# The first gather of a mixture-of-experts layer reads unscaled rows, and a ninth weight unit is loaded into the room of the scaled copy

## What is computed

```python
h = x + merge_heads(...)                       # 288 tokens x 2048
xn = h * rsqrt(mean(h*h) + EPS) * g_ffn_norm   # rms_norm
g_sel = argmax(xn @ w_rg + b_rg)               # one of 4 groups
top_v, top_i = top_k(expert logits of that group, 2)
gate = g_prob * softmax(top_v)
for each expert e (32 of them), rows xb = xn[its tokens]:
    y[its tokens] += gate * ((silu(xb @ w_gate[e]) * (xb @ w_up[e])) @ w_down[e])
h = h + y
```

## Time and profile before

| | us |
|---|---|
| median of three runs | 1785.23 |
| the three runs | 1783.72, 1785.23, 1787.71 |
| the profiled execution, its own time | 1790.77 |
| its span, first to last instruction | 1789.1 |
| PE busy | 1434.1 (80%) |
| DVE busy | 473.3 (26%) |
| ACT busy | 206.5 (12%) |
| POOL busy | 83.3 (5%) |
| DMA moved | 555.31 MB, mean 310 GB/s |

### The profile page before, as it was taken

The page is one execution under the profiler, slowest core; times in us unless marked ns, Lnnn a source line. Parts: engine busy times, 40 slices in busy tenths (PEclk is TensorE's granted clock), DMA queues, the critical chain, the costliest instruction groups (busy, mean ns, idle before and its releaser), DMA issues.

```text
span 1789.1 us, 22896 instructions
## 1 busy us (share of the span) xinstructions
PE 1434.1 (80%) x9330; PEld 798.3 (45%) x9330; DVE 473.3 (26%) x1217; ACT 206.5 (12%) x478; POOL 83.3 (5%) x147
## 2 busy tenths in 40 slices
PE   7999999999999999998767665866576567666646
PEld 6877777776777454455332231412223113122111
DVE  3106674552135666203002011011020110200201
ACT  3010101002332222113000000000000000000000
POOL 2000000220001322000000000000000000000000
PEclk9999999999999999998888888888888878878868
DMA  7643244342258999853899999999999999999996
GB/s 258 193 122 98 72 139 141 123 138 80 71 174 304 379 399 378 303 214 141 334 425 420 428 425 427 429 429 429 430 429 429 429 429 429 429 428 429 428 427 224
DMA packets 120617, 555.31 MB, mean 310 GB/s; under 512 B 11839, under 2 KB 65184, under 8 KB 94752
## 3 DMA queue, kind: packets, MB, share of 16 engines
q1 hardware_dynamic: 112080, 517.75, 72.4%
q0 software_dynamic: 8464, 36.54, 5.7%
HBM read 545.32 MB, written 8.72 MB: 310 GB/s over the span
## 4 chain that ended last, share of the span: by engine, by line
PE 64%; DMA 29%; DVE 3%; issue 1%; ACT 1%; SPq 1%; POOL 1%; DVEq 0%; POOLq 0%; ACTq 0%
PE PS L1859 22%; PE PS L2439 16%; DMA arena<-in_w_up_e_dram 9%; DMA arena<-in_w_down_e_dram 9%; DMA arena<-in_w_gate_e_dram 8%; PE PS L2480 7%; PE PS L2297 4%; DMA arena<-in_cache_fox_k_dram 2%; PE PS L2279 1%; PE PS L1913 1%; PE PS L2211 1%; PE PS L2398 1%; PE PS L2414 1%; PE PS L1847 1%; DVE arena L1537 1%
## 5 line engine op out<-in xcount | busy, mean ns | idle before, releaser
L2439 PE MATMUL PS<-arena 128*32 128x512 f32 x1792 | 291.5, 733 | 194.5 <-DMA arena<-in_w_up_e_dram 125.6
L1859 PE MATMUL PS<-arena 128*128 128x288 f32 (+1 forms) x1728 | 445.2, 406 | 1.0 <-ACT arena L996 0.5
L1859 PEld LDWEIGHTS PS<-arena 128*128 128x128 f32 x1728 | 320.8, 191 | 93.6 <-issue 20.9
L2439 PEld LDWEIGHTS PS<-arena 128*32 128x32 f32 x1792 | 70.4, 131 | 406.5 <-issue 195.1
L2480 PE MATMUL PS<-arena 128*32 128x512 f32 x872 | 136.8, 708 | 117.1 <-DMA arena<-in_w_down_e_dram 117.1
L2439 PE MATMUL PS<-front,arena 128*32 128x512 f32 x256 | 145.8, 735 | 0.0
L2480 PEld LDWEIGHTS PS<-arena 128*32 128x32 f32 x872 | 36.9, 127 | 210.8 <-issue 119.8
L1773 DVE TENSOR_TENSOR arena<-arena,PS 128x512 f32<-128x512 f32 x8 | 5.5, 687 | 401.8 <-PE PS L2439 401.8
L1783 DVE TENSOR_TENSOR arena<-arena,PS 128x512 f32<-128x512 f32 (+1 forms) x96 | 65.6, 683 | 157.9 <-PE PS L2414 157.9
L2398 PE MATMUL PS<-arena 128*128 128x128 f32 x768 | 94.3, 283 | 1.7 <-DVE arena L1747 1.7
L2398 PEld LDWEIGHTS PS<-arena 128*128 128x128 f32 x768 | 90.5, 197 | 9.7 <-issue 7.5
(11 more groups left out here) (365 smaller groups left out, 1291.6 us busy)
## 6 DMA issues: line engine op xcount, KB each, us to landing
arena<-in_w_gate_e_dram SPq DMA_DIRECT2D x56, 2048.0 KB, 15.0
arena<-in_w_up_e_dram SPq DMA_DIRECT2D x53, 2048.0 KB, 15.2
arena<-in_w_down_e_dram SPq DMA_DIRECT2D x53, 2048.0 KB, 15.3
arena<-in_cache_fox_v_dram POOLq DMA_DIRECT2D x64, 384.0 KB, 9.0
arena<-in_w_in_dram SPq DMA_DIRECT2D x6, 3072.0 KB, 10.8
front<-in_w_gate_e_dram SPq DMA_DIRECT2D x8, 2048.0 KB, 23.0
front<-in_w_up_e_dram SPq DMA_DIRECT2D x8, 2048.0 KB, 23.5
arena<-in_cache_fox_k_dram SPq DMA_DIRECT2D x40, 384.0 KB, 11.1
```

The lines of the kernel that those rows point to most:

```text
L1859: last = pe.matmul(PS[0:m, bank, 0:w], wt[:, k, c:c + m], rhs[:, k, :], start=(k == 0), stop=(k == KC - 1))
L2439: last = pe.matmul(PS[x * SLOTS:(x + 1) * SLOTS, which, :], xgT[:, kk, x * SLOTS:(x + 1) * SLOTS], wt[:, k, :], start=(kk == 0), stop=(kk ...
```

## The change

Five things are edited together.

1. The first gather (round 0) reads `h_tok` itself, in the strided order of `in_halves`, and multiplies it with `pick_first`, which is `pick_tok` times `rstd`. DVE makes it with three instructions right behind `pick_pair(0)`.
2. The scaled copy is made later, behind `units_used` 2: two instructions of ACT ahead of its first `pair_act`, one of DVE within `pair_dve(0)`. TensorE waits for them (`h_scl` 4) before it gathers for round 1.
3. The room of the copy, `HSC`, holds `ahead2` first, a ninth place for a unit, in which (1, 0) is loaded behind `wo_filled` 9. `pick_first` stands behind it.
4. The place that (1, 0) had is free, so (2, 1) is loaded into it at once, ahead of the wait on `half_used`, and no longer behind `units_used` 2.
5. POOL's clearing of tile 2 is gone, and every gather uses 32 rows of the third tile instead of 128.

```diff
+        ahead2 = view(HSC, UNIT)
+        pick_first = view(HSC + UNIT, 3, XQ, SLOTS)
...
             load_wo_rest(3, wo_in[2])
+            sp.wait_ge(wo_filled, 9)
+            sp.dma_start(ahead2.rearrange("p (k n) -> p k n", n=FFW), w_gate_r[0, 1]).then_inc(group_in[1], 16)
             sp.wait_ge(wo_filled, NWO)
-            for x in (0, 2):
-                load_first(1, x)
+            load_first(1, 2)
 
             sp.wait_ge(lg_filled, NWO)
             sp.dma_start(ahead.rearrange("p (k n) -> p k n", n=FFW), w_gate_r[1, 1]).then_inc(group_in[1], 16)
+            load_unit(0, 2, 1)
...
             for g in range(2, GROUPS):
-                for x in ((1,), (2, 3, 1), (0, 2, 3, 1), (0, 2, 3, 1))[g - 2]:
+                if g == 2:
+                    sp.wait_ge(units_used, g)
+                for x in ((), (2, 3, 1), (0, 2, 3, 1), (0, 2, 3, 1))[g - 2]:
...
-            pool.wait_ge(wo_filled, 9)
-            pool.memset(h_scaled[:, 2, :], 0.0).then_inc(consts_set, 1)
...
-            scale_rows(0, P)
-            scale_rows(1, P)
             for n, (o, i) in enumerate(((rw[:, :, 0:NG], rw[:, :, 0:NG]), (rw[:, :, 60:61], rw[:, :, 60:61]))):
...
+            act.wait_ge(units_used, 2)
+            scale_rows(0, P)
+            scale_rows(1, P)
             with act.Fori(0, QUADS - 1) as p:
                 pair_act(p)
...
-            dve.wait_ge(consts_set, N_CONSTS + 1)
-            dve.tensor_scalar(by_half(h_scaled[0:NS, 2, :]), in_halves(h_tok[0:NS, 2, :]), rstd[0:NS, 7:8], None, ALU.mult).then_inc(h_scl, 1)
...
+            def first_picks_scaled():
+                dve.wait_ge(picked_set, 1)
+                for t in range(3):
+                    ins = dve.tensor_scalar(pick_first[:, t, :, :], pick_tok[:, t, :, :], rstd[:, 5 + t:6 + t], None, ALU.mult)
+                ins.then_inc(h_scl, 1)
...
                 if not last:
                     dve.wait_ge(pg_set, p + 1)
                     pick_pair(p + 1)
+                if first:
+                    dve.wait_ge(units_used, 2)
+                    dve.tensor_scalar(by_half(h_scaled[0:NS, 2, :]), in_halves(h_tok[0:NS, 2, :]), rstd[0:NS, 7:8], None, ALU.mult).then_inc(h_scl, 1)
...
             pick_pair(0)
+            first_picks_scaled()
             gate_values()
...
-            def gather(p, chunks):
+            def gather(p, chunks, now=False):
 
                 for c in chunks:
                     o = PS[:, 2 + c // 4, (c % 4) * P:(c % 4 + 1) * P]
-                    for t in range(3):
-                        last = pe.matmul(o, h_scaled[:, t, c * P:(c + 1) * P], pick_tok[:, t, :, :].rearrange("p x s -> p (x s)"),
-                                         start=(t == 0), stop=(t == 2))
+                    for t, (t0, w) in enumerate(TILES):
+                        if now:
+                            h, picks = in_halves(h_tok[0:w, t, :])[:, c // 8, c % 8, :], pick_first
+                        else:
+                            h, picks = h_scaled[0:w, t, c * P:(c + 1) * P], pick_tok
+                        last = pe.matmul(o, h, picks[0:w, t, :, :].rearrange("p x s -> p (x s)"), start=(t == 0), stop=(t == 2))
...
-                                wt = ahead if first and (g, x) == (1, 1) else group_unit(g, x)
+                                wt = {(1, 1): ahead, (1, 0): ahead2}.get((g, x), group_unit(g, x)) if first else group_unit(g, x)
...
                         if g == 2 and not last_pair:
                             pe.wait_ge(picked_set, p + 2)
-                            if not first:
+                            if first:
+                                pe.wait_ge(h_scl, 4)
+                            else:
                                 pe.wait_ge(part_added, p * NPART)
                             gather(p + 1, range(8))
...
-            pe.wait_ge(picked_set, 1)
-            pe.wait_ge(h_scl, 3)
-            gather(0, range(5))
+            pe.wait_ge(h_scl, 1)
+            gather(0, range(5), True)
```

More of the change, by code:

```diff
@@ L2424, in pair_pe @@
                         if first and g == 1:
-                            gather(0, range(9, KC))
+                            gather(0, range(9, KC), True)
                         pe.wait_ge(group_in[g % 3], p * 128 + (64 * (g // 3) + 64))
@@ L2432, in pair_pe @@
                                 last.then_inc(half_used, 1)
-                                gather(0, range(5, 9))
+                                gather(0, range(5, 9), True)
                             if first and which == 0 and k % 4 == 0:
```

## The result

The changed kernel takes 1801.26 us in the median of six runs (1800.18 to 1804.35), the kernel before 1786.29 (six runs, the three from before the change among them): ratio 1.0086, 95% interval 1.0073 to 1.0099. It is slower by some 15 us where 7.4 us less were forecast, and outside the range. The profiled execution has a span of 1802.7 us against 1789.1.

The account below looks back on a forecast made before the run. Experts' weights stream at memory speed, 428 to 430 GB/s, while TensorE waits. One unit less (4.9 us) and a closed gap (3.1) make 8.0; with later events 7.4 remain, so 1785.23 - 7.4 = 1777.8 us, range 1776 to 1786.

Parts of the forecast that it names:

- 9.9 - c: Gain in us once C holds the stream of weight loads; the forecast c of 2.5 gave 7.4.
- c: Delay of event C caused by the change, forecast as 2.5 us.
- C: Event on TensorE when group 1 is done, 872.99 us in the kernel before, on which loads hang; forecast at 875.5.
- The gap closes: Before group 3's loads: (3, 1) is issued while earlier loads still come, so 3.1 us of idle stream go.
- the copy is covered: Before round 1's gather: ACT's late scalings, 7.97 us, delay nothing, as group 3's unit comes 5 us after that gather.
- TensorE need not stop after C: Between groups 1 and 2: with (2, 1) already loaded, group 2 follows directly and ends near 882 instead of 892.68.
- rival 3: At group 3's end: the gap opens one group later, up to 3 us lost again, 1781 us; chance 0.08.
- I take the pace as 0.147: First gather's strided load and matmul pairs: 0.147 us each, adding 0, 0.8 and 1.4 us in the three sets.
- sign of being wrong: Third set of first gathers, 42 strided loads: taking 10 us or more, where about 6.2 was forecast.
- rival 2: First gather's strided loads: 0.25 us each loses 0.6 us (1785.8), 0.294 a pair loses 4.9 (1790.1); chance 0.16.
- 1 (a load that does not hide): All 96 strided loads of the first gather: 0.093 us more per pair, c = 9.2, time 1784.5; chance 0.22.
- A: Event on TensorE when half of group 0 is done, 854.48 us in the kernel before, on which loads hang; forecast 0.3 later.

Follow-up runs that it names:

- E1: Changed kernel, but the first gather reads 128 neighbouring columns of h_tok (round 0 multiplies permuted rows): 1788.12 us, ratio 1.0005 to the kernel before.
- F2: Changed kernel, columns still 32 bytes apart, but with 128 rows of the third tile: 1786.75 us, ratio 0.9993 to the kernel before.
- F1: E1 with all 128 rows of the third tile in every gather: 1779.17 us, ratio 0.9945 to the kernel before.
- F3: Kernel before with 32 rows instead of 128 for the third tile in every gather, nothing else: 1794.9 us, ratio 1.0032.
- F4: F1 with round 0's weight rows placed to match contiguous columns of h_tok, gain applied in that order: 1782.74 us, ratio 0.9965 to the kernel before.
- E3: Changed kernel with the first gather's columns 8 bytes apart (round 0 multiplies permuted rows): 1790.27 us, one run.
- E4: Changed kernel with the first gather's columns 16 bytes apart (round 0 multiplies permuted rows): 1798.32 us, one run.
- G2: F4 with two neighbouring weight rows in a partition (4 KB pieces) and columns 8 bytes apart: 1782.81 us, ratio 0.9970 to the kernel before.

## Why the prediction was wrong

**The stream, the ninth unit and the formula were right.** Gain = 9.9 - c gives -14.2 for the c of 24.05, and the time rose by 15.0. For E1 the profile's C is 8.8 us later, counted from the first gather; with the 0.6 us of later start the formula gives a gain of 0.5, measured a loss of 0.9 with an interval that reaches to a gain of 0.7. For F2 it gives 0.1, measured about 1.2. With gathers as quick as before the sum of the prediction is 4.9 + 3.1 = 8.0, and F1 gained 8.5. "The gap closes" and "the copy is covered" hold in F1, and "TensorE need not stop after C" within 0.6 us (C at 872.16, group 2 at 872.78); the cover is gone in E1, whose gather for round 1 is slow.

One margin in the prediction mixes two counts: the "4.2 us" that the group before had in rival 3 leave out the 1.66 us from event to flow, which the two microseconds beside it include; with them it is 2.6. The time does not hang on it.

**Three steps failed, and all are terms of c.**

1. *"The third tile's 32 rows instead of 128 change no column count, so nothing."* This is the step that no rival covered. By itself it takes 8.9 us of C (E1 against F1) and 5.7 to 7.2 us of the time in the kernel before (F3). Of the 8.9 the half group behind the first set and the small matmul are 2.1, at the low clock of point 3. I priced the instruction and not the sequence: the gathers alternate between two forms, and before each change of form the loads stand still (0.22 us at half clock, F3).

2. *"I take the pace as 0.147."* Measured 0.24 at 128 rows (F2): 9.3 us of C where 2.2 were forecast. The third set in the changed kernel took 13.50 us, beyond the 10 that the prediction named as its sign of being wrong. Rows 6 were the wrong neighbour. They are a transpose, whose load is shorter to begin with (140 ns against 192), at 24 bytes. Near the mark was ScalarE's 0.25, the first price of rival 2, at the same 32 bytes and from the same tensor. I had that row, called it a bound and gave it 0.16 together with a worse one. Overlap of loads with matmuls, on which I leaned, is real at 113 ns; a strided load of 335 ns still comes every 243 ns (F2), so part of it is hidden and more than the forecast is not.

3. *The clock was no term at all.* The prediction took the half groups between the sets as fixed. After the change they took 6.05 and 6.12 us for the 3.6 of before, at a granted clock of 0.59 and 0.58 on average, 0.50 for the most part, with PE fully "busy". Summed: the sets give (10.19 - 6.46) + (7.47 - 2.99) + (13.50 - 4.89) = 16.8 us of c, the two half groups (6.05 - 3.57) + (6.12 - 3.64) = 5.0, group 1 1.3, the small matmul between (L2523) 0.4, and the later start 0.6: 24.1 in all. Taken one at a time stride and rows give 9.3 and 8.9, 18.2 together, but both at once 23.6 (52.2 - 28.6). Of the 5.4 us over their sum 4.6 lie in the half groups and group 1, which take (6.05 - 5.28) + (6.12 - 3.57) + (8.36 - 7.07) more than in E1, at the low clock. So either edit alone, contiguous columns (E1) or 128 rows (F2), gives back 14 to 15 us of c. In F2 the clock was 1.00 from 848 on, with pairs of 0.24 us; with pairs of 0.31 it fell again during the second and third sets.

In E1 and F3, with no stride, the clock stayed at 0.50 through the first set, at 0.31 us a pair, and once it was at 1.00 the second and third sets kept it at 0.176. In every profile whose clock stayed down through the first set, or fell in the second or third, the gathers have the 32-row form; no run has pairs of 0.31 us with 128 rows. So slow pairs and the form itself are not told apart, and the cause in the chip stays open. What it cost is measured.

Of the rivals, 1 (a load that does not hide) had a price of 0.093 more per pair and 1784.5; the stride costs 0.13. Rival 2 had the right place, the 66 loads between A and C, and nearly the right first price, but gave 1785.8, a loss of 0.6 us, because it lacked terms 1 and 3; F2, with these two out, measures level with the kernel before (0.9993). Its second price, 0.294 a pair, gave 1790.1, nearer to 1801.26, but by a double reading of the operand that F2's 0.24 does not bear out. The point it named, c = 9.9, is where F2 and E1 stand, and both measure as no change.

## What to carry to other kernels

Price what a change does to the sequence of forms on TensorE, not only each instruction: cutting the third tile's operand from 128 rows to 32 made every chunk of six pairs 0.35 us longer at full clock, and padding with zeros was faster. Where a stationary operand would be read more than 8 bytes apart in float32, give the slowest strided read of the same tensor on any engine a good chance as its price (one match here: ScalarE's 0.25 us, TensorE's 0.24), or change the row order of the other operand (F4) so that the read is contiguous. And where a stream of loads hangs on three events of one engine, the gain is bounded while the loss is not: here 8 us could be won and each further microsecond on that engine was paid nearly in full (c 24.05, time 15.0 up, against 9.9 - c).

## What the runs showed of the hardware that was not expected

- Changing between loads of 128 and of 32 rows leaves 0.22 to 0.23 us idle at each change at 1.2 GHz (F3). At 2.4 GHz an estimate is 0.18, half of the 0.35 that a chunk with two changes is longer.
- A stationary float32 operand with columns 8 bytes apart costs 0.007 us per 128 columns (E3), at 32 bytes it costs 0.13 (F2), and at 16 bytes the third set is as long as at 32 (13.54 and 13.50 us, E4 and the changed kernel).
- The granted clock was 0.50 over 12 us in which PE counts as busy all the time and no engine was waited for: "busy" in a window says nothing of the clock.
- Pieces of 2 KB came at 387 GB/s, of 4 KB at 404 and of 8 and 16 KB at 417 in the same window (F4, G2, F1), against 428 in the long stretch.
